# First block's attention: paired scores in four banks, rows turned in the mix bank, fewer top-k rounds per unit

## The reference

```
o_a = sliding_window_sink_attn(...)   # 8 heads of 64, 2 key heads, window 128, a sink per head
o_b = indexer_sparse_attn(...)        # 4 heads of 64; each query sees the 128 keys of highest index score
o_c = mla_attn(...)                   # 4 heads, keys of 64 + 32 = 96 features, causal
mix = concatenate([o_a, o_b, o_c]);  x = layer_norm(ALPHA*x + mix @ w_out);  x = layer_norm(ALPHA*x + moe(x))
```

## Time and profile before

| what | us |
|---|---|
| median of 3 runs (lowest to highest) | 3533.27 (3529.2 to 3545.81) |
| profiled execution, span from first to last instruction | 3530.0 |
| TensorE busy | 3327.5 (94%) |
| VectorE busy | 1944.8 (55%) |
| ScalarE busy | 1391.3 (39%) |
| GpSimd busy | 396.0 (11%) |
| layer 0's attention, from the mask step of unit 2 to the last row scaling | 113.1 |
| mean granted clock of TensorE | 0.971 |

### The profile page before, as it was taken

The page is one execution under the profiler, slowest core; times in us unless marked ns, Lnnn a source line. Parts: engine busy times, 40 slices in busy tenths (PEclk is TensorE's granted clock), DMA queues, the critical chain, the costliest instruction groups (busy, mean ns, idle before and its releaser), DMA issues.

```text
span 3530.0 us, 42246 instructions
## 1 busy us (share of the span) xinstructions
PE 3327.5 (94%) x14912; PEld 2604.5 (74%) x14912; DVE 1944.8 (55%) x3038; ACT 1391.3 (39%) x2064; POOL 396.0 (11%) x241
## 2 busy tenths in 40 slices
PE   8899999998999989999988999999999999999998
PEld 6667777676777777888866888877887767668886
DVE  5765777567557765545374544465354443465353
ACT  4453566444536664222223222232223444432121
POOL 3101122330012223000000000010001000010000
PEclk9999999999999999999998999999999999999999
DMA  3101699321017993223313222323232212023232
GB/s 124 45 1 60 220 321 321 123 75 34 12 61 254 323 310 102 86 95 92 99 41 91 72 97 93 101 84 130 90 100 103 90 36 72 25 66 102 89 100 73
DMA packets 174980, 389.60 MB, mean 110 GB/s; under 512 B 11312, under 2 KB 70064, under 8 KB 174192
## 3 DMA queue, kind: packets, MB, share of 16 engines
q1 hardware_dynamic: 173424, 377.45, 32.9%
q0 software_dynamic: 1408, 10.23, 0.8%
HBM read 381.34 MB, written 6.29 MB: 110 GB/s over the span
## 4 chain that ended last, share of the span: by engine, by line
PE 68%; DVE 13%; DMA 8%; ACT 4%; DVEq 3%; issue 2%; POOL 1%; POOLq 0%; ACTq 0%; SPq 0%
PE ps L549 19%; PE ps L551 18%; PE ps L550 18%; DMA gate_up_stage<-in_w_gu 8%; DVE moe_lo L1907 4%; PE ps L699 3%; PE ps L666 2%; ACT moe_hi L1113 2%; PE ps L721 2%; PE ps L705 1%; PE ps L803 1%; PE ps L769 1%; ACT w_hi L1113 1%; PE ps L657 1%; DVE w_lo L1537 1%
## 5 line engine op out<-in xcount | busy, mean ns | idle before, releaser
L1537 DVE TENSOR_TENSOR w_lo<-w_stage,w_hi 128x1024 fp32r<-128x1024 f32 (+3 forms) x310 | 398.4, 1287 | 850.1 <-ACT w_hi L1113 849.2
L549 PE MATMUL ps<-xs_hi,w_hi 128*128 128x512 f32 (+2 forms) x1952 | 778.5, 399 | 45.5 <-DVE w_lo L1537 15.1
L1113 ACT ACTIVATE w_hi<-w_stage 128x1024 fp32r<-128x1024 f32 (+3 forms) x350 | 382.1, 1093 | 1023.9 <-PE ps L551 1010.4
L551 PE MATMUL ps<-xs_hi,w_lo 128*128 128x512 f32 (+2 forms) x1952 | 772.2, 396 | 0.0
L550 PE MATMUL ps<-xs_lo,w_hi 128*128 128x512 f32 (+2 forms) x1952 | 771.8, 395 | 0.0
L549 PEld LDWEIGHTS ps<-xs_hi,w_hi 128*128 128x128 f32 (+2 forms) x1952 | 369.2, 189 | 147.3 <-issue 28.0
L551 PEld LDWEIGHTS ps<-xs_hi,w_lo 128*128 128x128 f32 (+2 forms) x1952 | 369.1, 189 | 85.6
L550 PEld LDWEIGHTS ps<-xs_lo,w_hi 128*128 128x128 f32 (+2 forms) x1952 | 370.0, 190 | 83.2
L1907 DVE TENSOR_TENSOR moe_lo<-gate_up_stage,moe_hi 128x1024 fp32r<-128x1024 f32 x224 | 270.0, 1248 | 116.9 <-ACT moe_hi L1113 116.7
L1113 ACT ACTIVATE moe_hi<-gate_up_stage 128x1024 fp32r<-128x1024 f32 x224 | 226.1, 1054 | 139.4 <-DMA gate_up_stage<-in_w_gu 131.9
L551 PE MATMUL ps<-h_hi,w_lo 128*128 128x512 f32 x704 | 278.1, 395 | 0.0
(11 more groups left out here) (366 smaller groups left out, 5006.7 us busy)
## 6 DMA issues: line engine op xcount, KB each, us to landing
gate_up_stage<-in_w_gu SPq DMA_DIRECT2D x112, 1024.0 KB, 5.5
w_stage<-in_f_gu SPq DMA_DIRECT2D x174, 512.0 KB, 3.5
down_stage<-in_w_dn SPq DMA_DIRECT2D x112, 512.0 KB, 5.8
w_stage<-in_f_dn SPq DMA_DIRECT2D x64, 704.0 KB, 4.0
w_stage<-in_w_in SPq DMA_DIRECT2D x30, 512.0 KB, 3.7
w_stage<-in_d_qk SPq DMA_DIRECT2D x24, 512.0 KB, 3.5
w_stage<-in_w_out SPq DMA_DIRECT2D x16, 512.0 KB, 3.6
w_stage<-in_d_v SPq DMA_DIRECT2D x12, 512.0 KB, 3.5
```

What stands on the lines that cost most here:

```text
L549: pe.matmul(o, lh, rh, start=start, stop=False)
L551: return pe.matmul(o, ll, rh, start=False, stop=stop)
L1113: copy = lambda o, i: nc.scalar.activation(o, i, ACT.Copy)
L1537: tt(w_lo[:, s, 0:n], stage[:, s, 0:n], w_hi[:, s, 0:n].bitcast(F32), ALU.subtract).then_inc(w_split, 1)
```

## The change

- `S_BANKS` has four banks (0 to 3) for three. Four scores are issued ahead of the loop for three. In an even turn n TensorE waits for the mask step of unit n + 1 and issues the scores of units n + 4 and n + 5, in an odd one none. Before it issued one in each turn, after the mask step of unit n.
- The rows of a batch are turned in the bank in which they were mixed, 6 + B%2, as bank 0 now holds scores. With it the wait for `ot_split` goes from the turning to the first mix of the batch after next; there it takes the place of the wait for `rows_ready`. Turning, high part and low part come one turn earlier.
- The 28 rounds are in other turns: before n = 0 to 30 except every fourth, then 32, 34, 36, 38; after the even n of 0 to 30, 9 and 25, and then 32, 33, 34, 36, 37, 38, 40, 41, 42, 44. The three operations that make the mask move from turn 39 to turn 45.

```diff
-        S_BANKS, S_RING = (2, 3, 1), 4
+        S_BANKS, S_RING = (0, 1, 2, 3), 4
...
                     if un is UN[0] or UN[n - 1]["last"]:
                         if un["B"] >= 2:
-                            pe.wait_ge(rows_ready, l * BATCHES + un["B"] - 1)
+                            pe.wait_ge(ot_split, l * BATCHES + un["B"] - 1)
...
                     pe.wait_ge(rows_ready, l * BATCHES + B + 1)
-                    if B > 0:
-                        pe.wait_ge(ot_split, l * BATCHES + B)
                     for i in range(nt):
-                        last = pe.transpose(ps[:, 0, i * P:i * P + P], rows_o[:, B % 2, i * P:i * P + P], ident[:, :])
+                        last = pe.transpose(ps[:, 6 + B % 2, i * P:i * P + P], rows_o[:, B % 2, i * P:i * P + P], ident[:, :])
...
-                for n in range(3):
+                for n in range(4):
                     scores(UN[n], n, S_BANKS)
...
-                    if n + 3 < N:
-                        pe.wait_ge(masked, c0 + n + 1)
-                        scores(UN[n + 3], n + 3, S_BANKS)
+                    if n % 2 == 0 and n + 4 < N:
+                        pe.wait_ge(masked, c0 + n + 2)
+                        for i in (n + 4, n + 5):
+                            scores(UN[i], i, S_BANKS)
                     if 0 <= n - 1 < N:
                         mix(n - 1)
-                    if n - 4 in LAST:
-                        turn_rows(LAST.index(n - 4))
+                    if n - 3 in LAST:
+                        turn_rows(LAST.index(n - 3))
...
-                    if n - 5 in LAST:
-                        B = LAST.index(n - 5)
+                    if n - 4 in LAST:
+                        B = LAST.index(n - 4)
...
-                ROUND_UNITS = ([n for n in range(32) if n % 4 < 3] + list(range(32, 48, 2)))[:len(rounds)]
+                ROUND_UNITS = [n for n in range(32) if n % 2 == 0 or n % 16 == 9] + [n for n in range(32, 45) if n % 4 < 3]
+                assert len(ROUND_UNITS) >= len(rounds) and ROUND_UNITS[len(rounds) - 1] < 45
+                ROUND_UNITS = ROUND_UNITS[:len(rounds)]
...
-                    if n - 7 in LAST:
-                        low(LAST.index(n - 7))
+                    if n - 6 in LAST:
+                        low(LAST.index(n - 6))
```

More of the change, by code:

```diff
@@ L1207, in attend @@
                         copy(xs_hi[:, ba["tiles"], ba["at"]:ba["at"] + P],
-                             ps[:, 0, 0:nt * P].rearrange("p (a n) -> p a n", n=P)).then_inc(ot_hi_done, 1)
+                             ps[:, 6 + B % 2, 0:nt * P].rearrange("p (a n) -> p a n", n=P)).then_inc(ot_hi_done, 1)
             def attend_wide(U, c0, hi_of):
@@ L1673, in mask_scores @@
                     init = 3.0e38 if un["sink"] is None else nsink[:, un["sink"]:un["sink"] + 1]
-                    V.tensor_tensor_reduce(prob[:, b, 0:W], ps[:, S_BANKS[n % 3], 0:W], un["mask"], -un["scale"], init, ALU.add, ALU.min,
+                    V.tensor_tensor_reduce(prob[:, b, 0:W], ps[:, S_BANKS[n % 4], 0:W], un["mask"], -un["scale"], init, ALU.add, ALU.min,
                                            nmax[:, un["B"] % 2, un["col"]:un["col"] + 1]).then_inc(masked, 1)
@@ L1708, in low @@
                     v.wait_ge(ot_hi_done, l * BATCHES + B + 1)
-                    tt(xs_lo[:, at[0], at[1]], ps[:, 0, 0:nt * P].rearrange("p (a n) -> p a n", n=P),
+                    tt(xs_lo[:, at[0], at[1]], ps[:, 6 + B % 2, 0:nt * P].rearrange("p (a n) -> p a n", n=P),
                        xs_hi[:, at[0], at[1]].bitcast(F32), ALU.subtract).then_inc(ot_split, 1)
```

## The result

The changed kernel takes 3507.66 us (median of 6 runs, 3503.96 to 3516.23), the kernel before in runs beside it 3536.16 (6 runs). The ratio is 0.9927, with a 95% interval of 0.9907 to 0.9947: 26 us less (19 to 33; the medians differ by 28.5), faster by more than the 0.5% that can be told apart. The forecast was 3515 in 3505 to 3530. The profiled execution has a span of 3510.8 us against 3530.0, 19.2 less, and its own time of 3512.6 is one of the slower of the six.

The account below looks back on a forecast made before the run. VectorE was taken to pace turns 8 to 31, TensorE to bound the stretch from turn 46. Layer 0's -13.2 and layer 1's -11.5 us, with +6 for low clock, took 3533.3 to 3515, range 3505 to 3530.

Parts of the forecast that it names:

- turns 0 to 7: First stretch of layer 0's attention: a mask step goes into VectorE's wait and two of six rounds leave, -3.0 us.
- turns 8 to 31: Stretch paced by VectorE: 14 rounds instead of 18, -6.8 us, with 0.3 us per batch given back, -5.9.
- turns 32 to 45: Stretch where VectorE had room: ten rounds instead of four, +2.9 us, and a later mix of unit 44, +0.2.
- from turn 46: Last stretch, bound by TensorE: 7 visits to the 64-row score form instead of 15, -7.4 us.
- low clock, on top: TensorE's gaps were to bring 8 us more at half clock per layer, costing 3 us each, +6 in all.
- no clock cost: Rival: VectorE paces the stretches where TensorE idles, so slow matmuls hide; 3509 us, 20%.
- Pairs run side by side: 64-row scores of two neighbours in different row halves cost one visit where they cost two, saving 0.39 us plus the columns.
- The thinning: Rounds spread thinner: -6.8 us on VectorE in turns 8 to 31, +9.4 in turns 32 to 45, leaving +2.9 there.
- The new wait: First mixes at units 36, 40, 44 wait for an earlier low part; TensorE stands 2 to 3 us, mostly covered, +0.2.
- the clock takes half of the gain: Rival: the low clock level reaches beyond turn 45, where each microsecond costs half of one; 3521 to 3527 us, 17%.
- slower: Last rival: new wait and low clock feed each other in turns 32 to 45 and after, 19.1 us per layer; 3546, 10%.
- ScalarE and the emptying of PSUM: Rival: one of these becomes the bound from turn 46 and half of the 7.4 us stays away; 3522 us, 8%.

Follow-up runs that it names:

- e4: Changed kernel, but both 64-row scores of a pair read rows 0 to 63, the same half; 3516.78 us, ratio 0.9960 to the kernel before.
- e3: Changed kernel, but one unit's scores issued in each turn, four units ahead, so no pair stands together; 3546.36 us, ratio 1.0041 to the kernel before.
- e6: Changed kernel with clock keepers also in the latent attention, in each turn 32 to 47; 3511.75 us, ratio 0.9927 to the kernel before.
- e1: Changed kernel with the 28 rounds in the turns they had before, so pairs only; 3509.47 us, ratio 0.9930 to the kernel before.
- e7: Changed kernel with seven rounds moved to turns 46 to 56 and the last query block's mask to turn 57; 3485.02 us, ratio 0.9860.
- e5: Changed kernel with the low part ahead of the round in VectorE's turn; 3507.51 us, ratio 0.9927 to the kernel before.
- e10: The changed kernel once more, nothing altered, for a second profile; 3506.25 us, ratio 0.9931 to the kernel before.
- e11: Changed kernel with one unit's scores in each turn, run again for a second profile; 3527.77 us, ratio 1.0009 to the kernel before.

## Why the prediction was right, point by point

| step | forecast, us | layer 0 | layer 1 |
|---|---|---|---|
| turns 0 to 7 | -3.0 | -2.8 | -2.8 |
| turns 8 to 31 | -5.9 | -7.0 | -5.9 |
| turns 32 to 45 | +3.1 | +4.6 | +4.6 |
| from turn 46 | -7.4 | -6.7 | -0.4 |
| low clock, on top | +3 | in the rows above | in the rows above |
| sum | -10.2 | -11.8 | -4.6 |

(Layer 1's forecast sum was 1.7 smaller.)

The time itself is in part luck. Of the forecast's 18.7 us (24.7 less 6) the profiled attentions gave 16.3, and the rest of the measured 26 came from elsewhere or from executions without a trace. At 3507.66 the time lies outside the forecast's own band of 3510 to 3520 and beside the rival *no clock cost*, 3509, which the trace refutes: the clock did cost, as below.

**Pairs run side by side.** Right, and shown: the earlier trace rows already had it in three units, e4 undoes it and gives 4.0 + 1.0 us back in layer 0. The fixed price of a visit, 0.39 us, was about right too: from turn 46 of layer 0 e3 takes 32.5 us, e4 29.6 and the changed kernel 25.6, so the joined visit is worth 2.9 and the overlap 4.0 of the 7 us; the sum of rows had 3.1 and 4.3. These are lengths of single profiled executions, all at clock 1.00.

**The thinning.** Right as a shift: -6.8 of rounds in one stretch and +9.4 in the next, of which +2.9 was to be left; e6, which has turns 32 to 45 at clock 1.00, measures 27.5 us against 24.5, +3.0. e1 shows that it carries nothing beside pairs. The room left after turn 45 was in the earlier trace rows (VectorE busy 12.2 of 32.2 us) but I did not draw from it that the rounds stood in the wrong place; e7 does.

**The new wait.** Its place was right, its length was not. TensorE's timeline after, turns 34 to 37 of layer 0:

```profile
200.83 0.66 PE L729 MATMUL ps<-ident,rows_o 128*128 128x128 f32 x4 [1.85 <-DVE rows_o L1703]
...
202.78 2.69 PE L699 MATMUL ps<-k_c,q_c 96*128 96x384 f32 x4 [0.43 <-DVE neg_max L1675]
...
207.29 1.12 PE L721 MATMUL ps<-v_c,prob_t 128*128 128x64 f32 x4 [1.07 <-DVE xs_lo L1710]
```

It stops for 1.85 us before turning rows and 1.07 before a mix; 2 to 3 us were forecast for the mix of units 36, 40 and 44, and the trace has 1.07 us at the first and under 0.3 at the other two (0.84, under 0.3 and 1.19 in layer 1). The stop before the turning after unit 31 stands in no term of the forecast; it was looked for only after units 7 and 23 (1.09 and 1.46 us there, 1 to 2 forecast). The pair of scores at 202.78 takes 2.49 us, nearly all at half clock, which fills what would have been idle. e5 takes the round out of the wait and shortens turns 32 to 45 by 0.4 us only in layer 1 and 1.4 in layer 0: the wait is nearly covered for VectorE, as stated. At turn 45 the mix of unit 44 starts 0.39 us later against VectorE's mask step than in the kernel before (224.77 against 224.63, where it was 229.75 against 230.00); 0.2 was forecast. What the forecast did not see is that this wait is on TensorE's path: with the mask scalings behind the low part (e5) the last stretch is 1.4 us shorter at the same full clock.

**The clock** is the term that was most mis-sized. It stood at 3 us per layer. In layer 0, turns 32 to 45 took 29.1 us at 0.77, and e6 27.5 at 1.00, so 1.6 us. In layer 1 the last stretch alone lost 6.3 us, and turns 8 to 31 another 1.0 (37.1 us at 0.95 against 36.1). The low clock from turn 46 is what the rivals *the clock takes half of the gain* and *slower* were about, in one layer of two, but it did not reach over from turns 32 to 45. Layer 1 of the changed kernel, by stretches of one level each, and TensorE's stop between the second and the third:

```profile
892.60:902.80 10.20, 9.27 (x27) 6.04 (x27) 9.36 (x27) 4.75 (x16) 0.00 (x0) 0.50 0.00 1
902.80:914.30 11.50, 10.45 (x72) 8.00 (x71) 10.18 (x28) 7.96 (x21) 0.00 (x0) 1.00 0.01 2
914.30:916.30 2.00, 1.86 (x16) 1.61 (x16) 1.01 (x7) 0.77 (x3) 0.00 (x0) 1.00 0.00 0
917.00:929.00 12.00, 12.00 (x52) 9.65 (x53) 3.34 (x14) 4.86 (x20) 0.00 (x0) 0.50 0.00 0
```

```profile
914.44 1.10 PE L721 MATMUL ps<-v_c,prob_t 128*128 128x64 f32 x8 [1.19 <-DVE xs_lo L1710]
```

The clock was back at 902.8 and fell again at 916.4, 2.0 us behind a stop of 1.19 us, and this stop is the new wait: the mix of unit 44 waits for the low part that stands behind the mask scalings. e10's layer 1 has the same stop of 1.19 us and the same fall 2.0 us behind it, e11's a stop of 0.91 and the fall 2.1 us behind it. With the low part first (e5) the stop is 0.62 us and no fall follows, in either layer; nor does one follow e10's stop of 0.66 us in layer 0. So new wait and low clock do go together, in a place that the forecast counted with 0.2 us and no clock. That the stop alone brings the clock down is not shown: in the kernel before, a stop of 0.90 us (ended at 218.94) was followed by none. In layer 0 of the changed kernel TensorE came to turn 45 late, after low clock until 216.8, hardly stopped there, and kept its full clock. e11 goes further than the last rival in its last stretch (25.5 us lost in a kernel with single visits) and not as far before it (27.5 us at 0.88 in turns 32 to 45).

**The rest of the program.** The forecast moved it along unchanged. By the two profiles of the changed kernel it is 2.8 and 7.8 us shorter than in the one of before (3305.5, against 3302.7 and 3297.7). The attentions gave less than the forecast, so what took the time 7 us under it must lie there or in executions that were not profiled. This part runs from 3293.0 to 3307.1 us over all profiles with the same instructions in it, so a single profile can't say whether the change had a hand in it. Some of it is the clock: behind layer 1's attention the kernel before took 2576.7 us with 135 at 0.50, the changed kernel 2564.7 with 86 and 2567.9 with 89. Why is left open.

**ScalarE and the emptying of PSUM** did not bind: ScalarE is busy 18.3 of 25.6 us from turn 46, and e5 reaches 24.2 us with TensorE busy 24.2 of them (24.8 forecast). The rule of the Trainium skill ("TensorEngine Tiling (Array Packing)", PSUM Bottleneck), that the emptying may become the bound once the tiles are packed, did not show in this trace. What e7 shows is something else: seven rounds, which empty nothing, stand in VectorE's order before the steps that do; VectorE is busy 22.0 of 29.9 us, TensorE 26.6, and the stretch is 5.7 us longer than e5's.

## What to carry to other kernels

Where two matmuls contract 64 rows and their operands lie in different row halves, issue them one behind the other into different banks: the second was free here. Before filler work of one engine is spread more thinly, lay the engines' busy times side by side for every stretch, and put the filler where the other engine is the bound; moving it between the stretches that its own engine bounds gave nothing here (e1), and moving some of it out gave 22 us, part of it through the clock (e7). When one engine's work shrinks, expect TensorE's gaps to grow, and look at its clock in the stretch behind: what TensorE waits for belongs ahead of filler work in the other engine's order. In e5 that shortened the attentions by 11 us in the trace, though not the median.

## What the hardware showed that was not expected

- The low clock can outlast the idle time that came before it by far. In e11 it stayed at 0.50 for all but the first 2 us of a stretch of 57.6 us, with TensorE busy 57.4 of them by the trace, while the same instructions in layer 0 ran at 1.00 in 32.1 us. The work is small matmuls of 64 to 512 columns with a weight load each.
- It can fall anew in the midst of busy work: at 916.4 us of the changed kernel TensorE had been busy for the 2.0 us since a stop of 1.19 us, and for 10.45 of the 11.5 us before, all at 1.00.
- Clock keepers can hold the level (e6, 1.00 in layer 0's turns 32 to 45), but they are paid where TensorE is the bound (27.1 us from turn 46 against 25.6 without them).
- Two matmuls of different row halves took no measurable time more than one: 1.06 us for two units of 512 columns, 1.06 for one.
